# An encoder block with 16384 single-neuron experts: a store moved two loads forward in SyncE's order, and four loads moved from ScalarE's queue to SyncE's

## The chip, the cores and the metric

The kernel runs on one core of a Trainium2 chip. The metric is the device time of one execution in microseconds (us). Each engine of the core works through its own list of instructions in order: TensorE (PE), VectorE (DVE), ScalarE (ACT), GpSimd (POOL) and SyncE (SP). SP computes nothing here; it only waits on semaphores and issues transfers (DMAs), one after the other. A row "SPq" is a transfer's issue on SP, "ACTq" one on ACT's queue.

## What is computed

256 tokens of width 1024 go through one bidirectional encoder block: an input projection, two token mixers (differential attention and neighbourhood attention), gates and an output projection, and then a feed-forward part (PEER) in which every token picks 128 of 16384 experts, each a single neuron. Some seven tenths of the span (793 of 1100 us) go into the feed-forward part, and the change lies there:

```python
def peer_ffn(x, w_query, sub_keys, expert_u, expert_v):
    ...
        q = (xb @ w_query).reshape(TB, PH, 2, PEER_QUERY_DIM // 2)
        s = jnp.einsum('thpd,hpkd->thpk', q, sub_keys).astype(jnp.float32)
        v_half, i_half = lax.top_k(s, K)
        ...
        g = jax.nn.softmax(top_s, axis=-1).astype(xb.dtype)
        u = expert_u[idx]
        a = jax.nn.gelu(jnp.einsum('td,thkd->thk', xb, u), approximate=False)
        return jnp.einsum('thk,thkd->td', g * a, expert_v[idx])
```

The kernel does not gather. It computes gelu(x u) for all 16384 experts, spreads the gates g over a dense matrix G (token by expert, mostly zeros), multiplies the two, and multiplies the product with all of expert_v.

## The kernel before

Weights come in tiles of 128 x 1024 float32 (512 KB), one after the other: 72 tiles of the projections, then 128 tiles of expert_u (here U tiles 0 to 127; in the code t = T_U + i, with T_U = 72), then 128 of expert_v (V tiles). A product of full precision is made of three rounded ones. So each tile passes four stations:

- SP loads it into one of four buffers `raw` (`load`, line 343; it waits until `lo_ready` says that the tile four places earlier has been split, which frees the buffer).
- ACT rounds it into `whis` (`hi`, line 436; a buffer of four, free when PE has finished the tile four places earlier).
- POOL (up to U tile 17) or DVE (from U tile 18: `low_u`, line 883) subtracts to get the remainder `wlos` and raises `lo_ready`.
- PE multiplies: 24 matmuls of 128 x 256 for a U tile, into one of two PSUM banks `pO`.

After a U tile, ACT applies Gelu from `pO` into `ast`, which has two buffers (`gelu`, line 543). SP stores `ast` to the scratch tensor `a_scratch` in HBM (`store`, line 364; it waits for that Gelu by `evac_act`). From the third tile on, `gelu(i)` waits until the store of tile i-2 has landed (`a_stored`), since it writes the same buffer. PE's tile i+2 in turn needs the bank that `gelu(i)` empties.

G is built between the U tiles 39 and 123, in 64 steps on three tiles of every four (`g_step_at`, line 91; `G_LAST` = 123). DVE makes one-hot vectors (`one_hots`, lines 941 and 946), ACT scales a copy of them (`low_hots`, line 561), PE adds two short matmuls after the first half of the tile's chunks and two after the second (`g_tokens`, line 1246), ACT copies the sum from PSUM (line 581) and DVE adds its second half (`add_low`, line 953). On ACT the order within tile i is: `hi(i+3)`, `low_hots`, `gelu(i)`, the copy, `low_hots`. On DVE it is: `one_hots` for the next step, `add_low` of the last step, `low_u(i+2)`, `one_hots`.

SP's order in the U loop is written out: load of tile t, then the store of tile t - `STORE_LAG`, which is 7 (lines 370 to 377). Each waits in turn, so a store cannot go before the load that stands ahead of it.

In the V loop the stored activations come back: `aring`, four buffers, loaded from `a_scratch`. The first four of these loads stand on ACT's queue behind U tile 123 (`first_weights`, line 550), the others on SP's behind each V load (`load_a`). DVE multiplies one with its column of G (`weights`, line 958), ACT rounds the product (`w_hi`, line 597) and DVE takes the remainder (`low`, line 963, `glo_ready`). PE's V tile needs both, and its 12 matmuls of 128 x 512 add into four accumulators. `aring` lies where the buffers of the G steps lay before, so it may only be loaded when these are done.

Of the kernel before, what the change touches and what calls it, by code (L numbers as in the profile page):

```python
# [61 lines left out]
NE_TILES = NK  # L62
# [1 line left out]
T_END = T_V + NE_TILES  # L64
RAW = 4
RING = 4
STORE_LAG = 7
LEAD = 3

UNROLL = 8  # L70
# [6 lines left out]
G_STEPS = T // GTOK  # L77
G_FIRST = 39
G_LAST = G_FIRST + (G_STEPS - 1) // 3 * 4 + (G_STEPS - 1) % 3
# [11 lines left out]
def g_step_at(i):  # L91

    at = i - G_FIRST
    if at < 0 or at % 4 == 3:
        return None
    k = at // 4 * 3 + at % 4
    return k if k < G_STEPS else None
# [40 lines left out]
def act_takings(t):  # L138

    return sum(not evac_engine(x)[0] for x in range(t))  # L140


def build(nc, stream, vrows, const, cols, keys, bias, lamv, gfin, h1_dram, a_dram, out):
    with ExitStack() as top:
# [3 lines left out]
        def sem(name):  # L148
            return top.enter_context(nc.semaphore(name))

        def sbs(stack, name, shape, dt=F32):
            return stack.enter_context(nc.sbuf_tensor(name, shape, dt))
# [71 lines left out]
        with ExitStack() as vphase:  # L224
# [5 lines left out]
            aring = [sbs(vphase, f"aring{s}", [P, T]) for s in range(4)]  # L230
# [79 lines left out]
        g_done = sem("g_done")  # L310
        g_copied = sem("g_copied")
        a_stored = [sem(f"a_stored{s}") for s in range(2)]
        a_landed = [sem(f"a_landed{s}") for s in range(4)]
# [15 lines left out]
        def _(sp):  # L329
# [13 lines left out]
            def load(t, s, row):  # L343

                sp.wait_ge(lo_ready, t - RAW + 1)
                sp.dma_start(raw[s][:], row).then_inc(raw_landed[s], 16)
# [17 lines left out]
            def store(i, s2):  # L364

                sp.wait_ge(evac_act, i + (act_takings(T_U) + 1))
                sp.dma_start(a_dram[i] if isinstance(i, int) else a_dram[bass.ds(i, 1)], ast[s2][:]).then_inc(a_stored[s2], 16)


            for t in range(T_U, T_V):  # L370
                load(t, t % RAW, stream[t])
                if t >= T_U + STORE_LAG:
                    store(t - T_U - STORE_LAG, (t - T_U - STORE_LAG) % 2)
            for s in range(RAW):
                load(T_V + s, s, vrows[s:s + 1])
                i = NE_TILES + s - STORE_LAG
                store(i, i % 2)

            def load_v(i, s):

                row = vrows[i] if isinstance(i, int) else vrows[bass.ds(i, 1)]
                sp.wait_ge(lo_ready, i + (T_V - RAW + 1))
                sp.dma_start(raw[s][:], row).then_inc(raw_landed[s], 16)
# [6 lines left out]
            for s in range(RAW):  # L390
                load_v(RAW + s, s)
                i = NE_TILES + RAW + s - STORE_LAG
                if i < NE_TILES:
# [41 lines left out]
        def _(act):  # L435
# [11 lines left out]
            def hi_at(t):  # L447
                if t < T_END:
                    hi(t, t % RING, landings(t))
# [78 lines left out]
            def take_scores(hp):  # L528

                act.wait_ge(key_scores, hp + 1)  # L530
                act.activation(sc[:, :, hp, :], pS[hp % 2][:, 0:TB * NK].rearrange("p (b k) -> p b k", b=TB), ACT.Copy).then_inc(sbank_taken, 1)
# [11 lines left out]
            def gelu(i):  # L543

                act.wait_ge(tile_done, T_U + i + 1)
                if i >= 2:
                    act.wait_ge(a_stored[i % 2], 16 * (i // 2))
                act.activation(ast[i % 2][:], pO[i % 2][:, 0:T], ACT.Gelu).then_inc(evac_act, 1)  # L548

            def first_weights(s):  # L550

                act.wait_ge(a_stored[s % 2], 16 * (s // 2 + 1))
                act.dma_start(aring[s][:], a_dram[s]).then_inc(a_landed[s], 16)

            def low_hots(u):

                act.wait_ge(hots_ready, u + 1)
                last = None
                for tok in range(GSUB):
                    at = u * GSUB + tok  # L560
                    last = act.activation(ghot[:, u % HOTS, tok, 1, :], ghot[:, u % HOTS, tok, 0, :].bitcast(F32), ACT.Copy,  # L561
                                          scale=routeT[:, 2, at:at + 1])
                last.then_inc(low_hots_ready, 1)

            def u_tile(i):
                hi_at(T_U + i + LEAD)
                ahead = g_step_at(i + 1)
                if ahead is not None:
                    low_hots(2 * ahead)
                if i < 2:  # L570
                    take_scores(HP - 2 + i)
                gelu(i)
                if i == EXP_AT:
                    act.wait_ge(pick_max, 1)
                    act.activation(route[:, :, 2, :, :], route[:, :, 2, :, :], ACT.Exp).then_inc(pick_exp, 1)
                    act.preload_act_table(ACT.Gelu)
                k = g_step_at(i)
                if k is not None:

                    act.wait_ge(g_done, k * 2 + 2)  # L580
                    act.activation(G[:, k * GTOK:(k + 1) * GTOK, :],  # L581
                                   pG[k % 2][:].rearrange("p b (t h i) -> p (b t) h i", t=GSUB, h=2)[:, :, 0], ACT.Copy).then_inc(g_copied, 1)
                if ahead is not None:
                    low_hots(2 * ahead + 1)

            for i in range(G_LAST + 1):
                u_tile(i)

            for s in range(4):
                first_weights(s)  # L590

            def w_hi(i, s):

                act.wait_ge(w_ready, i + 1)
                if not (isinstance(i, int) and i < 2):
                    act.wait_ge(tile_done, i + (T_V - 1))
                act.activation(ghi[s % 2][:], wfull[s % 2][:], ACT.Copy).then_inc(ghi_ready, 1)  # L597

            for i in range(G_LAST + 1, NE_TILES):
                u_tile(i)  # L600
                if i >= NE_TILES - 2:
                    w_hi(i - NE_TILES + 2, i - NE_TILES + 2)
# [784 lines left out]
```

## Time and profile before

| | |
|---|---|
| time, median of 3 runs (lowest to highest) | 1102.28 us (1102.02 to 1104.24) |
| the profiled execution's own time | 1101.85 us |
| its span, first to last instruction | 1100.0 us |
| mean granted TensorE clock | 0.985 |
| busy: PE, PE weight loads, DVE, ACT, POOL | 94%, 86%, 78%, 54%, 20% |
| DMA | 195 GB/s over the span, queue q1 (SP's) 59.6% of 16 engines |
| longest entry of the chain that ended last, beside PE's V loop | DMA a_scratch<-ast, 16% |

The span has four parts: projections, mixers and queries up to 307 us; U tiles without G steps from 307 to 421 us; U tiles with G steps from 421 to 721 us, with the last four U tiles to 734 us; the V loop from 734 us to the end. The matmuls of PE overlap and their ends are modelled, so PE's pace is better read from the distance between the starts of two tiles than from its busy share. A time is read from the profiled execution; what lies around its span is 1.85 us, and its own time is 0.43 us below the median of the runs.

### The profile page before, as it was taken

To read this page: it belongs to the slowest core of one execution; us is meant where nothing else is said; L and a number is where in the kernel's file an instruction comes from. 1 tells how busy PE (TensorE), PEld (TensorE's weight loads), DVE (VectorE), ACT (ScalarE), POOL (GpSimd) and SP (SyncE) were. 2 spreads that over 40 slices of the span, in tenths; PEclk is the share of its full clock that TensorE was granted. 3 is DMA by queue.
4 is the path that set the end of the run, shared out by engine and by line. 5 is a ranking of instruction groups with operands and counts; after the bars stand their busy time and mean duration, and the time that the engine had idled before them with its cause. 6 is when DMAs were issued, how large, how long until landed. Compare 5 with 4: busy or idle time off the path is not lost.

```text
span 1100.0 us, 20666 instructions
## 1 busy us (share of the span) xinstructions
PE 1039.1 (94%) x6950; PEld 943.9 (86%) x6950; DVE 852.8 (78%) x1658; ACT 594.5 (54%) x1089; POOL 218.9 (20%) x94
## 2 busy tenths in 40 slices
PE   5898899889999999999999999999999999999997
PEld 5787899889999999999899899888888888888885
DVE  6988552747999898888788888867777777777776
ACT  5234444254444445777677777755444555444553
POOL 3565556666776000000000000000000000000000
PEclk8899999989999999999999999999999999999999
DMA  8333324444567675665656566688677766776772
GB/s 295 111 135 116 115 97 151 137 174 152 203 195 236 197 244 167 186 190 192 192 183 188 182 195 191 181 256 302 233 239 234 231 231 236 236 236 235 232 230 82
DMA packets 86453, 215.00 MB, mean 195 GB/s; under 512 B 9712, under 2 KB 42864, under 8 KB 85872
## 3 DMA queue, kind: packets, MB, share of 16 engines
q1 hardware_dynamic: 85808, 213.54, 59.6%
q8 instruction: 45, 0.74, 0.3%
q10 hardware_dynamic: 576, 0.52, 0.2%
q14 instruction: 24, 0.20, 0.1%
HBM read 195.15 MB, written 18.87 MB: 195 GB/s over the span
## 4 chain that ended last, share of the span: by engine, by line
PE 51%; DVE 20%; DMA 17%; ACT 8%; issue 3%; SPq 1%; ACTq 0%; DVEq 0%
PE pTT L1297 16%; PE pM L1297 16%; DMA a_scratch<-ast 16%; PE pO L1053 15%; DVE wlos L885 3%; ACT G L581 2%; ACT whis L441 2%; ACT ghot L561 2%; DVE qkT L740 1%; DVE G L953 1%; ACT ast L548 1%; DVE biasm L783 1%; DVE nmx L762 1%; DMA iota<-in_count 1%; DVE mfull L809 1%
## 5 line engine op out<-in xcount | busy, mean ns | idle before, releaser
L441 ACT ACTIVATE whis<-raw 128x1024 fp32r<-128x1024 f32 x328 | 344.6, 1051 | 47.0 <-PE pO L1053 40.6
L422 POOL TENSOR_TENSOR wlos<-raw,whis 128x1024 fp32r<-128x1024 f32 x89 | 218.5, 2461 | 131.7 <-ACT whis L441 131.6
L1053 PE MATMUL pO<-xhi,whis 128*128 128x256 f32 x704 | 200.7, 285 | 3.8 <-ACT ast L548 3.8
L967 DVE TENSOR_TENSOR wlos<-raw,whis 128x1024 fp32r<-128x1024 f32 x125 | 153.2, 1226 | 59.4 <-ACT whis L441 59.4
L1053 PE MATMUL pO<-xhi,wlos 128*128 128x256 f32 x704 | 198.5, 282 | 0.0
L1053 PE MATMUL pO<-xlo,whis 128*128 128x256 f32 x704 | 198.1, 281 | 0.0
L597 ACT ACTIVATE ghi<-wfull 128x256 fp32r<-128x256 f32 x128 | 53.5, 418 | 175.4 <-PE pM L1297 175.4
L885 DVE TENSOR_TENSOR wlos<-raw,whis 128x1024 fp32r<-128x1024 f32 x113 | 137.3, 1218 | 11.1 <-ACT whis L441 11.0
L1272 PE MATMUL pO<-xhi,whis 128*128 128x256 f32 x512 | 143.5, 280 | 1.1 <-ACT ast L548 1.0
L1272 PE MATMUL pO<-xlo,whis 128*128 128x256 f32 x512 | 143.3, 280 | 0.0
L1272 PE MATMUL pO<-xhi,wlos 128*128 128x256 f32 x512 | 143.1, 279 | 0.0
L1053 PEld LDWEIGHTS pO<-xhi,whis 128*128 128x128 f32 x704 | 133.7, 190 | 5.7 <-issue 5.3
L1053 PEld LDWEIGHTS pO<-xlo,whis 128*128 128x128 f32 x704 | 134.0, 190 | 0.0
L1053 PEld LDWEIGHTS pO<-xhi,wlos 128*128 128x128 f32 x704 | 133.7, 190 | 0.0
L548 ACT ACTIVATE ast<-pO 128x256 f32<-128x256 f32 x128 | 48.9, 382 | 139.9 <-DMA a_scratch<-ast 109.5
L1272 PEld LDWEIGHTS pO<-xhi,whis 128*128 128x128 f32 x512 | 96.1, 188 | 1.8 <-issue 1.8
L1272 PEld LDWEIGHTS pO<-xlo,whis 128*128 128x128 f32 x512 | 96.3, 188 | 0.0
L1272 PEld LDWEIGHTS pO<-xhi,wlos 128*128 128x128 f32 x512 | 96.2, 188 | 0.0
L561 ACT ACTIVATE ghot<-ghot,routeT 128x128 fp32r<-128x128 f32 x256 | 88.2, 396 | 8.4 <-DVE ghot L946 8.4
L1053 PE MATMUL pO<-yhi,whis 128*128 128x256 f32 x256 | 78.8, 308 | 11.1 <-DVE ylo L649 8.4
L1297 PE MATMUL pTT<-whis,ghi 128*128 128x512 f32 x256 | 80.7, 395 | 0.0
L1297 PE MATMUL pM<-whis,ghi 128*128 128x512 f32 x256 | 80.6, 394 | 0.0
(187 smaller groups left out, 2055.5 us busy)
## 6 DMA issues: line engine op xcount, KB each, us to landing
raw<-in_stream SPq DMA_DIRECT2D x200, 512.0 KB, 3.7
raw<-in_vrows SPq DMA_DIRECT2D x128, 512.0 KB, 3.5
a_scratch<-ast SPq DMA_DIRECT2D x128, 128.0 KB, 3.8
aring<-a_scratch SPq DMA_DIRECT2D x124, 128.0 KB, 3.3
biasm<-in_bias SPq DMA_DIRECT2D x1, 2048.0 KB, 8.1
xT<-in_xTin SPq DMA_DIRECT2D x2, 512.0 KB, 6.0
keysT<-in_keys SPq DMA_DIRECT2D x1, 1024.0 KB, 5.6
h_scratch<-h1tok SPq DMA_DIRECT2D x1, 1024.0 KB, 6.5
```

The source lines that it names most:

```text
L422: pool.tensor_tensor(wlo[s], raw[s][:], whi[s].bitcast(F32), ALU.subtract).then_inc(lo_ready, 1)
L441: act.activation(whi[s], raw[s][:], ACT.Copy).then_inc(hi_ready, 1)
L548: act.activation(ast[i % 2][:], pO[i % 2][:, 0:T], ACT.Gelu).then_inc(evac_act, 1)
L561: last = act.activation(ghot[:, u % HOTS, tok, 1, :], ghot[:, u % HOTS, tok, 0, :].bitcast(F32), ACT.Copy, scale=routeT[:, 2, at:at + 1])
L581: act.activation(G[:, k * GTOK:(k + 1) * GTOK, :], pG[k % 2][:].rearrange("p b (t h i) -> p (b t) h i", t=GSUB, h=2)[:, :, 0], ACT.Copy).t ...
L597: act.activation(ghi[s % 2][:], wfull[s % 2][:], ACT.Copy).then_inc(ghi_ready, 1)
L740: dve.tensor_tensor(qkT[:, k, :], rtmp[:, 0, :], rtmp[:, 1, :], ALU.add).then_inc(roped, 1)
L885: dve.tensor_tensor(wlo[t % RING], raw[t % RING][:], whi[t % RING].bitcast(F32), ALU.subtract).then_inc(lo_ready, 1)
L967: dve.tensor_tensor(wlo[s], raw[s][:], whi[s].bitcast(F32), ALU.subtract).then_inc(lo_ready, 1)
L1053: last = pe.matmul(dst, st, mv, start=(c == 0 and q == 0), stop=(c == len(terms) - 1 and q == 2))
L1272: last = pe.matmul(pO[i % 2][:, 0:T], st[s][:, c, :], mv[:, c, :], start=c == 0 and q == 0, stop=c == C - 1 and q == 2)
L1297: last = pe.matmul(acc[b][q], st, mv[:, q * 512:(q + 1) * 512], start=first and n == 0, stop=final and n == 2)
```

## The change

`STORE_LAG` becomes 5, so the store of U tile i stands directly behind the load of tile i+5, two loads further forward than before. The four first loads of `aring` leave ACT's queue and stand on SP's, behind the store of U tile 123, with a wait for all G steps (`g_done`) ahead of them. The buffers, the sizes and the number of transfers stay.

```diff
-STORE_LAG = 7
+STORE_LAG = 5
...
                 i = NE_TILES + s - STORE_LAG
                 store(i, i % 2)
+                if i == G_LAST:
+
+                    sp.wait_ge(g_done, 2 * G_STEPS)
+                    for q in range(4):
+                        sp.wait_ge(a_stored[q % 2], 16 * (q // 2 + 1))
+                        sp.dma_start(aring[q][:], a_dram[q]).then_inc(a_landed[q], 16)
...
-            def first_weights(s):
-
-                act.wait_ge(a_stored[s % 2], 16 * (s // 2 + 1))
-                act.dma_start(aring[s][:], a_dram[s]).then_inc(a_landed[s], 16)
-
...
-            for i in range(G_LAST + 1):
-                u_tile(i)
-
-            for s in range(4):
-                first_weights(s)
-
...
-            for i in range(G_LAST + 1, NE_TILES):
+            for i in range(NE_TILES):
                 u_tile(i)
```

SP, at the start of the U loop, before (the rows are the loads of U tiles 4 to 7, the store of tile 0, the load of tile 8 and the store of tile 1; the number behind a name is the buffer):

```order
L346 DMA raw0<-in_stream 128x1024 [waits lo_ready]
L346 DMA raw1<-in_stream 128x1024 [waits lo_ready]
L346 DMA raw2<-in_stream 128x1024 [waits lo_ready]
L346 DMA raw3<-in_stream 128x1024 [waits lo_ready]
L367 DMA a_scratch<-ast0 128x256 [waits evac_act]
L346 DMA raw0<-in_stream 128x1024 [waits lo_ready]
L367 DMA a_scratch<-ast1 128x256 [waits evac_act]
```

SP at the same place, after:

```order
L346 DMA raw0<-in_stream 128x1024 [waits lo_ready]
L346 DMA raw1<-in_stream 128x1024 [waits lo_ready]
L367 DMA a_scratch<-ast0 128x256 [waits evac_act]
L346 DMA raw2<-in_stream 128x1024 [waits lo_ready]
L367 DMA a_scratch<-ast1 128x256 [waits evac_act]
L346 DMA raw3<-in_stream 128x1024 [waits lo_ready]
L367 DMA a_scratch<-ast0 128x256 [waits evac_act]
```

The store of tile 0 now follows the load of tile 5 instead of 7, and from there on load and store alternate with this smaller distance through all 128 tiles; the load of tile i+6 now stands behind the store of tile i.

SP, at the end of the U loop, before (from the load of V tile 0; the stores are those of U tiles 121 to 125, the row of L388 is the load of activation 4):

```order
L346 DMA raw0<-in_vrows 128x1024 [waits lo_ready]
L367 DMA a_scratch<-ast1 128x256 [waits evac_act]
L346 DMA raw1<-in_vrows 128x1024 [waits lo_ready]
L367 DMA a_scratch<-ast0 128x256 [waits evac_act]
L346 DMA raw2<-in_vrows 128x1024 [waits lo_ready]
L367 DMA a_scratch<-ast1 128x256 [waits evac_act]
L346 DMA raw3<-in_vrows 128x1024 [waits lo_ready]
L367 DMA a_scratch<-ast0 128x256 [waits evac_act]
L383 DMA raw0<-in_vrows 128x1024 [waits lo_ready]
L367 DMA a_scratch<-ast1 128x256 [waits evac_act]
L388 DMA aring0<-a_scratch 128x256 [waits w_ready,a_stored0]
```

SP at the same place, after (the stores are those of U tiles 123 to 126):

```order
L346 DMA raw0<-in_vrows 128x1024 [waits lo_ready]
L367 DMA a_scratch<-ast1 128x256 [waits evac_act]
L383 DMA aring0<-a_scratch 128x256 [waits a_stored0,g_done]
L383 DMA aring1<-a_scratch 128x256 [waits a_stored1]
L383 DMA aring2<-a_scratch 128x256 [waits a_stored0]
L383 DMA aring3<-a_scratch 128x256 [waits a_stored1]
L346 DMA raw1<-in_vrows 128x1024 [waits lo_ready]
L367 DMA a_scratch<-ast0 128x256 [waits evac_act]
L346 DMA raw2<-in_vrows 128x1024 [waits lo_ready]
L367 DMA a_scratch<-ast1 128x256 [waits evac_act]
L346 DMA raw3<-in_vrows 128x1024 [waits lo_ready]
L367 DMA a_scratch<-ast0 128x256 [waits evac_act]
```

The four loads of `aring` now stand between the store of U tile 123 and the load of V tile 1.

ACT around the end of U tile 123, before:

```order
L548 ACTIVATE ast1<-pO1 128x256 [waits a_stored1,tile_done]
L581 ACTIVATE G<-pTT 128x512 [waits g_done]
L553 DMA aring0<-a_scratch 128x256 [waits a_stored0]
L553 DMA aring1<-a_scratch 128x256 [waits a_stored1]
L553 DMA aring2<-a_scratch 128x256 [waits a_stored0]
L553 DMA aring3<-a_scratch 128x256 [waits a_stored1]
L441 ACTIVATE whis<-raw3 128x1024 [waits tile_done,raw_landed3]
L548 ACTIVATE ast0<-pO0 128x256 [waits a_stored0,tile_done]
```

ACT at the same place, after:

```order
L554 ACTIVATE ast1<-pO1 128x256 [waits a_stored1,tile_done]
L582 ACTIVATE G<-pTT 128x512 [waits g_done]
L447 ACTIVATE whis<-raw3 128x1024 [waits tile_done,raw_landed3]
L554 ACTIVATE ast0<-pO0 128x256 [waits a_stored0,tile_done]
L447 ACTIVATE whis<-raw0 128x1024 [waits tile_done,raw_landed0]
```

The four issues are gone from ACT, and nothing else there has moved (the line numbers shift by the length of the new code).

## Rows read from the trace of the kernel before

**Rows 1.** Busy time by stretch: length, then us (and count) by engine, clock, DMA, GB/s.

```profile
307.00:421.29 114.29, 112.16 (x949) 111.47 (x948) 105.49 (x302) 55.26 (x83) 37.04 (x16) 1.00 0.70 218
421.29:721.04 299.75, 284.39 (x2298) 274.27 (x2297) 248.74 (x530) 217.61 (x489) 0.00 (x0) 1.00 0.60 185
721.04:734.46 13.42, 11.72 (x99) 11.43 (x97) 6.91 (x8) 6.41 (x11) 0.00 (x0) 1.00 0.88 284
740.00:1080.00 340.00, 340.00 (x1459) 272.76 (x1458) 266.18 (x366) 169.46 (x244) 0.00 (x0) 1.00 0.71 238
```

**Rows 2.** Timeline of PE: starts of U tiles 58 to 62.

```profile
489.34 0.28 PE L1053 MATMUL pO<-xhi,whis 128*128 128x256 f32 x1
...
492.17 0.28 PE L1272 MATMUL pO<-xhi,whis 128*128 128x256 f32 x1
...
495.85 0.28 PE L1272 MATMUL pO<-xhi,whis 128*128 128x256 f32 x1
...
499.83 0.28 PE L1272 MATMUL pO<-xhi,whis 128*128 128x256 f32 x1
...
503.12 0.28 PE L1053 MATMUL pO<-xhi,whis 128*128 128x256 f32 x1
```

**Rows 3.** Waits of the engines, whole span: us in total, times, longest.

```profile
ACT ast L548 <- DMA a_scratch<-ast: 109.5, 79, 3.4
...
DVE G L953 <- ACT G L581: 53.9, 63, 3.1
```

**Rows 4.** Waits of SP's queue, whole span: us in total, times, longest.

```profile
SPq L346 <- DVE wlos L885: 277.5, 110, 6.9
...
SPq L367 <- ACT ast L548: 12.3, 33, 1.4
```

**Rows 5.** Chain that ended last, one turn: start, us, what.

```profile
449.31 0.60 ACT G L581
...
449.94 0.69 DVE G L953
450.63 1.14 DVE wlos L885
...
451.79 0.33 SPq L346
...
452.17 3.72 DMA a_scratch<-ast
```

**Rows 6.** Timeline of ACT and of SP: Gelu of tile 59, its store.

```profile
497.93 0.38 ACT L548 ACTIVATE ast<-pO 128x256 f32<-128x256 f32 x1 [1.00 <-DMA a_scratch<-ast]
498.21 0.59 ACT L581 ACTIVATE G<-pTT 128x512 f32<-128x512 f32 x1
498.69 0.69 ACT L561 ACTIVATE ghot<-ghot,routeT 128x128 fp32r<-128x128 f32 x2
...
501.06 0.43 SPq L367 DMA_DIRECT2D a_scratch<-ast  x1
```

**Rows 7.** Timeline of PE: start of U tile 23.

```profile
374.46 0.35 PE L1053 MATMUL pO<-xhi,whis 128*128 128x256 f32 x1 [1.29 <-ACT ast L548]
```

**Rows 8.** Timelines, end of the U loop: Gelu 125, U tile 127, glo, V tile 0.

```profile
730.86 0.38 ACT L548 ACTIVATE ast<-pO 128x256 f32<-128x256 f32 x1 [3.43 <-DMA a_scratch<-ast]
...
731.39 0.36 PE L1053 MATMUL pO<-xhi,whis 128*128 128x256 f32 x1 [1.70 <-ACT ast L548]
...
733.82 0.42 DVE L963 TENSOR_TENSOR glo<-wfull,ghi 128x256 fp32r<-128x256 f32 x1 [0.37 <-ACT ghi L597]
...
734.39 0.47 PE L1297 MATMUL pTT<-whis,ghi 128*128 128x512 f32 x1
```

**Rows 9.** Issue to landing, 421 to 721 us: tile raw, then tile a_scratch.

```profile
DMA to landing us min/median/max: 3.6/3.7/4.9
...
DMA to landing us min/median/max: 3.5/3.7/5.3
```

**Rows 10.** Issues by line: the first loads of aring, KB each, us to landing.

```profile
aring<-a_scratch ACTq DMA_DIRECT2D x4, 128.0 KB, 3.1
```

## The prediction, made blind

> **What bounds the kernel now.** I read the busy times by stretch first [rows 1]. In the V loop PE is busy 340.00 of 340 us: nothing but PE counts there, and time won earlier is kept. In the stretch with G steps (421 to 721 us) matmuls are busy 284 of 300 us, which looks like a full engine. The tile starts say otherwise [rows 2]. Tile 58, without a G step, takes 492.17 - 489.34 = 2.83 us, and tile 61, with one, 503.12 - 499.83 = 3.29 us; tiles 59 and 60, of the same work as 61, take 3.68 and 3.98. Tile 58's 2.83 is 24 matmuls one every 0.118 us without a gap, and 61's four short matmuls add the rest; so 2.83 and 3.29 are PE's floor. The four tiles 58 to 61 take 503.12 - 489.34 = 13.78 us, their floor is 3 x 3.29 + 2.83 = 12.70.
>
> What PE waits for is found with the waits [rows 3]: the longest one of the stretch is ACT's, 109.5 us in 79 Gelus that waited for the store of the same `ast` buffer. PE hardly waits for Gelu itself; it waits for what ACT does behind it (the copy of G, the scaled one-hots), which starts late with it. Why the store is late stands in SP's own waits [rows 4]: the load ahead of it waited 277.5 us for DVE's split, the store 12.3 us for its Gelu. The chain shows the loop that this closes [rows 5]: copy of G 0.60, `add_low` 0.69, split of tile i+3 1.14, issue of load i+7 0.33, store i 3.72 until it has landed, and only then Gelu i+2. With the Gelu (0.38) and the gaps between them one turn takes 6.9 to 7.0 us for two tiles: that is the present pace, 13.8 to 14 us for four. Tile 59 in full [rows 6]: its Gelu ends at 498.31, its store goes at 501.06, 2.75 us later.
>
> **The store two loads earlier, with G steps.** Store i now stands behind load i+5, which waits for the split of tile i+1. DVE makes that two tiles before the split of i+3, so it is done before Gelu i. The store then goes as soon as the Gelu ends, and the 2.75 us are gone. What is left of the loop: Gelu 0.38, issue, landing 3.72, next Gelu; some 4.3 us for two tiles, against PE's floor of 2.83 + 3.29 = 6.12 or more. Even the longest landing, 5.3 us [rows 9], fits. The other loop (copy, `add_low`, split i+1, load i+5, store i, Gelu i+2) keeps its 7 us but now spans four tiles, of 12.70 us.
>
> So I ask what is late next. ACT: from the start of a Gelu to the start of the `ghot` pair is 498.69 - 497.93 = 0.76 us, the pair ends some 0.7 later [rows 6], so 1.5 to 1.7 us after a tile's end the one-hots for the next tile's second half are there; PE wants them after that tile's 24 matmuls, 3.05 us. DVE: 248.74 us of work for 85 tiles is 2.93 us per tile, ACT 217.61/85 = 2.56 [rows 1], against a mean floor of 3.18. DVE would be 92% busy. In order on DVE, three G tiles in a row cost a little more than PE's floor and the fourth gives it back; its split of tile i+2 stays over 3 us ahead of PE. So PE is the bound and the stretch comes to its floor: 64 x 3.29 + 21 x 2.83 = 270.0 us instead of 299.75 [rows 1]. **Gain 29.8 us.** A lower end comes from PE's weight loads, idle 299.75 - 274.27 = 25.5 us.
>
> The Trainium skill ("Perfetto Trace Analysis", section Identifying the Most-Contended Engine) says the same of the measures: weight-load busy time shows TensorE's headroom and matmul busy time does not. By it the sum would have 25.5 us here, by matmul busy time 15.4; the tile starts of this trace say 29.8, and I go by them.
>
> **The store two loads earlier, before the G steps.** From 307 to 350 us nothing waits for stores for long. From 353 us on DVE's routing work delays splits, stores go late, Gelus with them, and PE waits for the bank, as tile 23 does, 1.29 us [rows 7]. With the store behind its Gelu this goes; ACT's two table loads near tile 20 are then the one thing there that comes close to PE. Weight loads are idle 114.29 - 111.47 = 2.8 us in this stretch [rows 1]. **Gain 2.8 us**, bounds 0 and 2.8.
>
> **What the moved store puts behind itself.** Load i+6 waited for a split alone; it now stands behind store i, hence behind Gelu i. Before 350 us this makes it nearly a tile (2.83 us) later. It is issued about 1 us after the end of tile i (Gelu 0.38, store issue 0.43, gaps), lands 3.7 us later, at most 4.9 [rows 9], and ACT rounds it after tile i+2, 5.7 us after tile i. With the longest landing the rounding is some tenths late, and PE wants the tile three tiles after that. With G steps the split and the Gelu come at about the same time, so the load hardly moves. **Cost 0.** SP issues 0.33 + 0.43 us per tile, far below 3.18.
>
> **The four loads on SP.** ACT loses four issues, which are not on PE's path: 0. On SP they wait for `g_done`, which tile 123 raises before its own Gelu is over, so this wait is met when the store of tile 123 goes. Behind them in SP's order stand the load of V tile 1 and the stores from 124 on: later by four issues, about 1.7 us at the store's 0.43. The first product of DVE needs `aring` 0: issue some 0.9 us after tile 123's end, landing after 3.1 us on ACT's queue [rows 10], longer behind a load, so by 4 to 5.5 us; ACT rounds that product after tile 126, about 9 us. PE's V tile 0 needs `glo` 0: Gelu 126, the rounding and DVE's 0.42 end about 1.4 us after tile 126, and tile 127 takes 2.83. Before, `glo` 0 started at 733.82 for a V tile 0 at 734.39 [rows 8]: the margin is small today since the Gelus are late, and grows. **Cost 0**, at most the 1.7 us.
>
> **The last four U tiles.** Gelu 125 waited for the store of 123 (it started at 730.86), and PE's tile 127 for that, 1.70 us [rows 8]. Four tiles should take 11.3; they took 734.39 - 721.04 = 13.35. **Gain 2.0 us.**
>
> **Sum.** 29.8 + 2.8 + 2.0 = 34.6 us, from the profiled execution's 1101.85: 1067.25; the median of the runs is 0.43 above it: 1067.7. That is the floor, and no row prices the small misses (a slow landing, an engine a tenth late). I add 1.3 us for them: **1069.0 us**.
>
> **Rivals.**
> - *DVE becomes the bound.* It is at 92% in the new pace, and today `add_low` waits 53.9 us for the copy, 0.86 per step [rows 3]. If half of that stays, DVE needs 248.7 + 27 us and with its other hand-offs some 280 for the stretch: 10 us less gain, **1078 us** (1073 to 1084). For it: three G tiles in a row are above PE's floor on DVE. Against it: the copy will follow PE's tile, not a store.
> - *Slower: loads starve behind the store.* If raw loads land late because SP waits for the Gelu first, a loop of six tiles closes: Gelu, store issue, load issue, landing, rounding, split, tile; some 6.9 us and the landing. It passes PE's floor (19.1 us for six) from a landing of 12.2 us, and today's pace (21.2) from 14.3; at 16 us the 85 tiles take 3.82 each and the kernel **1127 us**. Against it: the longest landing is 4.9 [rows 9]. The Trainium skill ("Perfetto Trace Analysis", section DMA Optimizations) speaks for it: it advises one engine for inputs and another for outputs, and this change ties them closer on one. No row here shows a harm from that.
> - *The handover gives back.* If `aring` or V tile 1 comes late, PE waits at 734 us for up to the four issues and a landing's spread: **1071 us**.
> - *It doesn't do what it says.* If the store still waits for the load ahead of it, as in today's rows, nothing changes: **1102 us**. The split of i+1 would have to be as late as that of i+3; the order on DVE excludes it.
>
> **Chances.** The floor with small misses (1067 to 1073) 0.66, DVE bound 0.22, handover 0.05, no change 0.03, loads starve 0.04. The range 1066.5 to 1079 holds the first, the third and over half of the second. About 0.2% (2.2 us) is what a measurement of this kernel can tell from no change: faster 0.93, same 0.03, slower 0.04.
>
> **What would show it.** In the profile after: a Gelu's wait for stores near nothing; the store's issue within 0.2 us of its Gelu; SP's stores, not its loads, waiting; tile starts 3.29 and 2.83 apart from 421 us on; V tile 0 at about 700 us; the V loop unchanged. It is wrong if four tiles still take over 13.2 us, and then the wait that PE's `g_tokens` or DVE's `add_low` shows names the cause; or if ACT's rounding waits for `raw`.

## The result and the profile after

| | before | after |
|---|---|---|
| time, median (lowest to highest), 4 runs each on one chip | 1103.12 us (1102.02 to 1104.24) | 1057.64 us (1055.03 to 1057.67) |
| ratio, 95% interval | | 0.9582 (0.9563 to 0.9601) |
| the profiled execution's own time | 1101.85 us | 1057.65 us |
| its span | 1100.0 us | 1055.8 us |
| mean granted TensorE clock | 0.985 | 0.989 |

The kernel became faster, as forecast, but by 44.2 us between the two profiled executions where the forecast's sum had 34.6 and the forecast itself 33. The time lies 9 us below the range.

Busy time by stretch of the kernel after (columns as in [rows 1]), cut at the starts of U tiles 0, 39 and 124 and of V tile 0:

```profile
306.44:417.66 111.22, 111.22 (x949) 111.22 (x948) 105.36 (x302) 55.35 (x83) 37.06 (x16) 1.00 0.68 222
417.66:679.58 261.92, 261.92 (x2298) 261.92 (x2297) 246.48 (x530) 220.68 (x490) 0.00 (x0) 1.00 0.65 215
679.58:690.47 10.89, 10.89 (x99) 10.89 (x98) 7.07 (x9) 6.16 (x10) 0.00 (x0) 1.00 0.81 272
697.00:1037.00 340.00, 340.00 (x1459) 273.95 (x1458) 265.15 (x365) 169.72 (x243) 0.00 (x0) 1.00 0.71 239
```

PE and its weight loads now fill each stretch of the U loop from end to end. Against [rows 1] and the tile starts of before, the stretch before the G steps went from 114.29 to 111.22 us (3.1 gained), that with them from 299.75 to 261.92 (37.8), the last four tiles from 13.35 to 10.89 (2.5). The V loop is as it was. The remaining 0.8 us lie ahead of tile 0 and in the tail.

Starts of U tiles 58 to 62 on PE after, for [rows 2]:

```profile
476.54 0.28 PE L1048 MATMUL pO<-xhi,whis 128*128 128x256 f32 x1
...
479.26 0.28 PE L1267 MATMUL pO<-xhi,whis 128*128 128x256 f32 x1
...
482.46 0.28 PE L1267 MATMUL pO<-xhi,whis 128*128 128x256 f32 x1
...
485.66 0.28 PE L1267 MATMUL pO<-xhi,whis 128*128 128x256 f32 x1
...
488.86 0.28 PE L1048 MATMUL pO<-xhi,whis 128*128 128x256 f32 x1
```

The tile without a G step takes 2.72 us and every one with a G step 3.20. Four tiles take 12.32 us, where they took 13.78, and where the forecast put PE's floor at 12.70. PE went below what the forecast called its floor. That is the surprise of this case.

The waits of the engines after (whole span; us in total, times, longest), for [rows 3]:

```profile
ACT ast L554 <- PE pO L1048: 69.5, 60, 2.0
...
ACT ast L554 <- PE pO L1267: 20.9, 41, 0.8
DVE G L948 <- ACT G L582: 16.2, 40, 2.1
...
ACT whis L447 <- DMA raw<-in_stream: 4.1, 4, 2.3
```

The Gelu's 109.5 us of waits for the store are gone: Gelu now waits for PE, as it should. `add_low` waits 16.2 us for the copy of G instead of 53.9. SP's queue (whole span), for [rows 4]:

```profile
SPq L367 <- ACT ast L554: 265.6, 128, 6.4
...
SPq L346 <- DVE wlos L880: 1.3, 4, 0.6
```

The waits have changed places. The store now waits for its Gelu (265.6 us, harmless), the load behind it for almost nothing: 1.3 us for DVE's split and, in the U loop, 2.8 us for POOL's. Tile 59 on ACT and SP, for [rows 6]:

```profile
482.42 0.38 ACT L554 ACTIVATE ast<-pO 128x256 f32<-128x256 f32 x1
482.70 0.60 ACT L582 ACTIVATE G<-pTT 128x512 f32<-128x512 f32 x1
...
482.83 0.34 SPq L367 DMA_DIRECT2D a_scratch<-ast  x1
483.22 0.43 SPq L346 DMA_DIRECT2D raw<-in_stream  x1
```

Its Gelu ends at 482.80 and the store goes at 482.83, 0.03 us later; it was 2.75. From issue to landing in the stretch with G steps, first the stores, then the raw loads, for [rows 9]:

```profile
DMA to landing us min/median/max: 1.7/2.2/3.3
...
DMA to landing us min/median/max: 3.4/3.9/5.5
```

The store lands in 2.2 us, where it took 3.7. The load behind it takes 0.2 us more. The handover, for [rows 8], on SP, DVE and PE:

```profile
679.95 0.34 SPq L367 DMA_DIRECT2D a_scratch<-ast  x1
680.41 1.81 SPq L383 DMA_DIRECT2D aring<-a_scratch  x4
...
689.66 0.42 DVE L958 TENSOR_TENSOR glo<-wfull,ghi 128x256 fp32r<-128x256 f32 x1
...
690.46 0.39 PE L1292 MATMUL pTT<-whis,ghi 128*128 128x512 f32 x1
```

The four loads of `aring` go right behind the store of tile 123 and take SP 1.81 us; `glo` 0 ends 0.38 us ahead of V tile 0, and PE has no gap there.

### The profile page after: what moved, and what is told of

Same layout as the page of the kernel before. It is cut to its first block, busy times and chain, and to the rows that moved or that the text cites. A ratio compares the mean times of both kernels' runs of the same rounds, so it can differ in the third digit from the quotient of the medians.

```text
span 1055.8 us, 20667 instructions
## 1 busy us (share of the span) xinstructions
PE 1010.9 (96%) x6950; PEld 928.6 (88%) x6950; DVE 848.7 (80%) x1658; ACT 597.7 (57%) x1089; POOL 218.9 (21%) x94
## 4 chain that ended last, share of the span: by engine, by line
PE 86%; DVE 10%; issue 1%; ACT 1%; DMA 1%; SPq 0%; DVEq 0%; ACTq 0%
PE pO L1048 30%; PE pTT L1292 17%; PE pM L1292 17%; PE pO L1267 17%; PE pTT L1241 1%; PE pSS L1241 1%; DVE qkT L735 1%; DVE nmx L757 1%; DVE biasm L778 1%; DMA iota<-in_count 1%; DVE mfull L804 1%; PE pM L1137 1%; DVE gates L655 1%; ACT prob L512 1%; PE pSS L1213 1%
## 5 line engine op out<-in xcount | busy, mean ns | idle before, releaser
L1048 PE MATMUL pO<-xhi,whis 128*128 128x256 f32 x704 | 198.8, 282 | 0.0
L1048 PE MATMUL pO<-xlo,whis 128*128 128x256 f32 x704 | 196.7, 279 | 0.0
L1267 PE MATMUL pO<-xhi,whis 128*128 128x256 f32 x512 | 141.3, 276 | 0.0
L1267 PE MATMUL pO<-xlo,whis 128*128 128x256 f32 x512 | 141.3, 276 | 0.0
L1292 PE MATMUL pTT<-whis,glo 128*128 128x512 f32 x256 | 80.7, 395 | 0.0
L1292 PE MATMUL pM<-whis,glo 128*128 128x512 f32 x256 | 80.7, 395 | 0.0
```

What stands on the lines that cost most here:

```text
L1048: last = pe.matmul(dst, st, mv, start=(c == 0 and q == 0), stop=(c == len(terms) - 1 and q == 2))
L1267: last = pe.matmul(pO[i % 2][:, 0:T], st[s][:, c, :], mv[:, c, :], start=c == 0 and q == 0, stop=c == C - 1 and q == 2)
L1292: last = pe.matmul(acc[b][q], st, mv[:, q * 512:(q + 1) * 512], start=first and n == 0, stop=final and n == 2)
```

## Experiments

Three questions: which half of the change brings the gain, by which loop of waits, and why PE went below the forecast's floor. All ratios are to the kernel before, run on the same chip beside each kernel. Where a stretch is named, its time is that of the profiled execution. Each edit is against the kernel after, unless it is said otherwise. In the 14 profiles tile 0 starts anywhere from 302.84 to 308.99 us, so single times of kernels with the same U loop can lie 6 us apart by what stands ahead of it.

### The loads of aring on SP alone

```diff
-STORE_LAG = 5
+STORE_LAG = 7
```

> The other half of the change alone: STORE_LAG 7, the four first aring loads on SP behind the store of tile 123. Theory: the G stretch is as in the kernel before; the aring loads now wait for a late store of tile 123, so DVE's first products come about 3 us later and V tile 0 starts 0 to 4 us later: 1102 to 1107 us. Rival (the move of the loads frees ACT and carries part of the gain beyond the forecast): 1090 to 1098 us.

Measured: 1104.97 us, ratio 1.0015 (0.9991 to 1.0039). Its waits (whole span; us in total, times, longest) are much like those of the kernel before:

```profile
ACT ast L554 <- DMA a_scratch<-ast: 124.8, 91, 3.3
DVE G L948 <- ACT G L582: 58.2, 64, 3.2
```

The second half of the change alone does nothing that can be measured.

### The store two loads forward alone

The first loads of `aring` stay on ScalarE's queue. Against the kernel before it is one number:

```diff
-STORE_LAG = 7
+STORE_LAG = 5
```

> The first half of the change alone: STORE_LAG 5, the four first aring loads on ACT's queue as before. Theory: all of the gain, within 1.5 us of the changed kernel (1056 to 1059). Rival (the move of the loads carries the 10 us beyond the forecast): 1066 to 1069 us.

Measured: 1056.85 us, ratio 0.9572 (0.9539 to 0.9606). Its waits of SP's queue (whole span) are those of the kernel after, and no Gelu waits for a store:

```profile
SPq L367 <- ACT ast L548: 274.7, 128, 6.4
...
SPq L346 <- DVE wlos L885: 1.1, 3, 0.6
```

The whole gain is the store's place. That the loads cost nothing on SP, as forecast, follows from this run and the one above.

### How far forward: six, four and three loads

Each is one number (with the few lines at the end of the U loop that keep the order whole):

```diff
-STORE_LAG = 5
+STORE_LAG = 6
```

> STORE_LAG 6 in the changed kernel, nothing else. Theory (loop): what counts is over how many tiles the 7 us loop copy of G, add_low, split, load, store, Gelu is spread; with 6 it is three tiles (9.1 us or more at PE's pace), so it does not bind, tiles with a G step start 3.2 us apart, and the time is within 2 us of the changed kernel (1057 to 1060). Rival (each place forward is worth its share): half of the gain, about 1080 us.

> STORE_LAG 4 in the changed kernel (the four aring loads again behind the store of tile 123), nothing else. Theory (loop): store i now holds back load i+5, whose rounding stands on ACT ahead of Gelu i+2. A loop closes over two tiles: Gelu 0.38, store issue 0.34, load issue 0.43, landing 3.9, rounding 1.05, some 6.2 us. Two tiles with G steps take 5.9 to 6.4 at PE's pace, two without 5.7: the tiles before 415 us become 3.1 us each, the others stay near 3.2 to 3.4; 1065 to 1085 us. Rival (earlier stores never hurt): 1057 us.

> The store of tile i stands three loads behind its own load instead of five, so SyncE issues it ahead of the load of tile i+4. Theory (the forecast's rival of a load that starves behind a store decides where a loop closes: store of i, load of i+4, halves of i+4, Gelu of i+4): over four raw buffers the load can't start before the store of tile i has been issued, which waits for Gelu i, so the halves of tile i+4 come at least landing 3.4 + rounding and difference about 2.3 us behind Gelu i, in which TensorE has only the tiles up to i+3 to do: it takes about one tile (Gelu i to halves i+4 to matmuls i+4 within four tiles, 4 x 2.72 = 10.9 us) and still closes, 1056 to 1075 us with TensorE waiting now and then. Rival (the order of the loads themselves is what limits): with the next load late by one more tile the U loop runs at 3.5 us or more a tile, 1140 us and above.

Measured: six, 1057.29 us, ratio 0.9585 (0.955 to 0.9621), the same as five. Four, 1074.16 us, ratio 0.9737 (0.9703 to 0.977). Three, 1425.82 us, one run. Three is a plain miss for what I wrote: the theory's 1056 to 1075 us is far off, and the rival's open "1140 us and above" holds the time only by the letter, since it was priced from 3.5 us a tile. Its waits (whole span), and one turn at three loads on SP and ACT:

```profile
ACT whis L447 <- DMA raw<-in_stream: 458.8, 127, 5.8
```

```profile
601.27 0.34 SPq L367 DMA_DIRECT2D a_scratch<-ast  x1
601.66 0.43 SPq L346 DMA_DIRECT2D raw<-in_stream  x1
...
605.37 1.06 ACT L447 ACTIVATE whis<-raw 128x1024 fp32r<-128x1024 f32 x1 [3.05 <-DMA raw<-in_stream]
...
606.91 0.36 ACT L554 ACTIVATE ast<-pO 128x256 f32<-128x256 f32 x1
...
607.30 0.34 SPq L367 DMA_DIRECT2D a_scratch<-ast  x1
```

The loop is one tile long, not four. Store i goes, then the load of tile i+4; it lands 3.71 us later; ACT rounds it, and the next Gelu stands behind that rounding in ACT's order; then the next store. One turn takes 607.30 - 601.27 = 6.03 us, and a tile with it: ACT's own order closes the loop long before PE does. (From 420 to 900 us of this run PE is busy 331 of 480 us and its granted clock averages 0.84. The turn shown has no wait for PE, so the clock does not set it.) This is the loop by which the change could have gone wrong. At three loads it spans one tile, at four two, at five three. Two tiles are 5.7 to 6.6 us at the paces of [rows 2], just at the 6.03 us; three are 8.2 us or more, so five loads leave over 2 us of room, and a sixth brings nothing more. (The room at five is worked out from this turn; no run made a landing longer.) At four the room is gone, as the waits of the stretch with G steps show (421.69 to 692.99 us):

```profile
ACT whis L446 <- DMA raw<-in_stream: 26.9, 47, 1.8
```

and the stretches of it:

```profile
306.12:421.69 115.57, 112.82 (x949) 111.90 (x948) 105.22 (x298) 55.75 (x82) 36.74 (x16) 1.00 0.70 213
421.69:692.99 271.30, 270.64 (x2298) 270.29 (x2297) 249.14 (x534) 223.20 (x490) 0.00 (x0) 1.00 0.67 208
```

The second row holds more than late loads. PE stands still only 0.66 us there by its busy time, and yet the stretch takes 9.4 us more than at five loads: its tiles take 2.83 and 3.29 us again where nothing is waited for. PE is busy; it is slower. A kernel further below, without a stop, takes 270.14 us for the same tiles at that pace, so some 8 of the 9.4 us are the pace and about 1 the late loads. (Of the other 7 us, 4.3 are in the stretch ahead and the rest behind it, where V tile 0 waits 1.34 and 0.70 us for `glo`.)

### Stores on ScalarE's queue

The Trainium skill, in the section that the forecast cites ("Perfetto Trace Analysis", section DMA Optimizations), says that it may make sense to give inputs one engine and outputs another. This kernel does so.

```diff
-                if t >= T_U + STORE_LAG:
-                    store(t - T_U - STORE_LAG, (t - T_U - STORE_LAG) % 2)
...
+                act.wait_ge(evac_act, i + (act_takings(T_U) + 1))
+                act.dma_start(a_dram[i], ast[i % 2][:]).then_inc(a_stored[i % 2], 16)
```

> The changed kernel, but every store of an activation tile is issued from ScalarE's queue, behind the Gelu that makes the tile; SyncE's queue then holds loads alone. Theory (what the change is worth is that the store goes at the Gelu's end and no longer behind a load's wait; which queue it has is not the point): the store goes as early, loads go earlier, but ScalarE gets an issue of 0.3 to 0.4 us a tile on top of 135.1 us of work per 52 tiles (2.60 us a tile); 2.9 to 3.0 against TensorE's mean 3.08 us leaves next to nothing, so some hand-offs come late: 1058 to 1080 us. [...]

Measured: 1057.60 us, ratio 0.9579 (0.9553 to 0.9604), the same as the kernel after, and just under the 1058 where my range began. Its DMA issues (KB each, median us to landing):

```profile
raw<-in_stream SPq DMA_DIRECT2D x200, 512.0 KB, 3.8
...
a_scratch<-ast ACTq DMA_DIRECT2D x128, 128.0 KB, 3.6
```

The loads no longer wait for a Gelu, the loop of the last section doesn't exist, and the time is the same: what limited the kernel before was the store that stood behind a load's wait. The three places tried that free it without closing a shorter loop (five loads, six loads, ACT's queue) are equally good, on one queue or on two. Neither harm nor gain of sharing a queue shows here.

### One stop of TensorE

In the stretch with G steps the trace of before has a stop of PE in nearly every round of four tiles, that of after none in the whole U loop. In the trace of before, a tile without a G step takes 2.83 us (24 matmuls at 118 ns) between those stops; in the trace of after 2.72 (113 ns). Both traces have 118 ns from tile 0 to tile 36 and 113 ns right behind the six transposes ahead of tile 37. Before goes back to 118 ns at its first stop behind them, at 428.8 us, and of the 128 groups of matmuls that can be read from there to 721 us one is at 113 ns. After stays at 113 ns to the end of the U loop. The granted clock is 1.00 in both. PE before, at the six transposes, the starts of tiles 38 and 39 (2.72 us apart) and that stop:

```profile
415.19 0.82 PE L1253 MATMUL pM<-cst,route 128*128 128x128 f32 x6
...
418.57 0.28 PE L1053 MATMUL pO<-xhi,whis 128*128 128x256 f32 x1
...
421.29 0.28 PE L1272 MATMUL pO<-xhi,whis 128*128 128x256 f32 x1
...
428.82 0.48 PE L1246 MATMUL pTT<-ghot,hot 128*128 128x256 f32 x2 [1.21 <-ACT ghot L561]
```

So the next edits stop PE in the kernel after, or put short matmuls ahead of a tile.

```diff
+            STOPS = (42,)
             for i in range(NE_TILES):
+                if i in STOPS:
+                    pe.wait_ge(evac_act, act_takings(T_U) + i)
```

> The changed kernel with one wait more: before U tile 42 TensorE waits until the Gelu of tile 41 has ended, so it stops once, early in the stretch with the G tiles. Theory (the pace of 113 ns from one matmul of 256 columns to the next, which the changed kernel has from tile 37 to the end of the U loop, is a state that lasts only while TensorE doesn't stop; after a stop it is drawn anew, and it came out at 118 ns after nearly all the stops of the kernel before): the stop itself costs 0.5 to 1 us, and if 118 ns is drawn the 82 tiles behind it cost 24 x 4.4 ns = 0.106 us each more, 8.7 us: 1066 to 1068 us, U tile starts 2.83 us apart. Rival (the pace belongs to the stretch, to what the other engines do there, and not to TensorE's own stops): 113 ns comes back at once, 1058 to 1059 us.

Measured: 1062.36 us median of 4 runs from 1059.89 to 1065.75, ratio 0.9621 (0.9589 to 0.9653). The profiled execution, at 1060.72, stopped once and kept 113 ns; of the 3.1 us that it lies above the kernel after, 2.6 stand ahead of tile 0 and 0.5 in the stretch with the stop. No forecast of mine covers the whole of it: the stop didn't bring back 118 ns in the run that I can see, and the two runs of 1064.00 and 1065.75 may have gone otherwise, which no trace shows. It doesn't tell the theories apart.

### Twelve stops, twice

```diff
+            STOPS = (6, 12, 18, 24, 30, 50, 60, 70, 80, 90, 100, 110)
```

> The changed kernel with twelve such waits, before U tiles 6, 12, 18, 24, 30 and 50, 60 up to 110: each stops TensorE until the Gelu of the tile ahead has ended. It samples the pace after a stop. Theory (drawn anew at a stop): the pace changes only at these places and at the six transposes ahead of tile 37, and both paces, 113 and 118 ns, are seen; twelve stops at 0.5 to 1 us are 6 to 12 us, and up to 60 slow tiles in place of fast ones 6 us, less what fast stretches ahead of tile 37 give back (up to 3 us): 1062 to 1076 us. Rival (the pace belongs to the stretch): 118 ns ahead of tile 37 and 113 ns behind it whatever the stops, 1064 to 1070 us.

> The kernel with twelve stops of TensorE once more, unchanged. Theory (the pace after a stop is drawn by chance in each execution): another pattern of 113 and 118 ns than the first profile had, where it was 118 behind tiles 6, 12, 24, 60, 80, 100 and the six transposes, and 113 behind 18, 30, 50, 70, 90, 110; time 1062 to 1076 us. Rival (the program determines the pace: the same instructions give the same pattern): the same pattern, 1065 to 1069 us.

Measured: 1067.08 us, ratio 0.9656 (0.9624 to 0.9688), and the same kernel again 1066.71, ratio 0.9665 (0.9624 to 0.9706). Both times lie in the ranges of theory and rival alike; only the profiles decide. PE in the first of the two profiles, at the stop ahead of tile 50 and the starts of tiles 54 and 55, then at the stop ahead of tile 60 and the starts of tiles 62 and 63:

```profile
456.74 0.38 PE L1048 MATMUL pO<-xhi,whis 128*128 128x256 f32 x1 [0.24 <-ACT ast L554]
...
469.17 0.28 PE L1048 MATMUL pO<-xhi,whis 128*128 128x256 f32 x1
...
471.89 0.28 PE L1270 MATMUL pO<-xhi,whis 128*128 128x256 f32 x1
...
487.81 0.38 PE L1270 MATMUL pO<-xhi,whis 128*128 128x256 f32 x1 [0.24 <-ACT ast L554]
...
494.51 0.28 PE L1048 MATMUL pO<-xhi,whis 128*128 128x256 f32 x1
...
497.34 0.28 PE L1270 MATMUL pO<-xhi,whis 128*128 128x256 f32 x1
```

The same tile, of the same stretch, takes 2.72 us behind one stop and 2.83 behind the next. Both paces exist on either side of tile 37. So the pace doesn't belong to the stretch: that rival falls. In both profiles it changed only at a stop or at the six transposes. The values behind tiles 6, 12, 18, 24, 30 were 118, 118, 113, 118, 113 in the first profile and 113, 118, 113, 118, 113 in the second; behind 50 to 110 they alternated from 113 in both. The same program gave two patterns ahead of tile 37 and one behind it: neither plain chance nor the program alone.

### Short matmuls without a stop

```diff
...
+            TURNS = {4: 1, 8: 2, 12: 3, 16: 4, 20: 5, 24: 6, 28: 1, 32: 2}
             for i in range(NE_TILES):
+                if i in TURNS:
+                    probe_turns(TURNS[i])
```

`probe_turns(n)` issues n idle transposes of 128 columns. In the second kernel it is three idle matmuls of 128 columns each, at the 16 tiles 4, 8 up to 32 and 50, 60 up to 120.

> The changed kernel with idle 128-column transposes put between U tiles, of which nothing comes: 1 ahead of tile 4, 2 ahead of 8, 3 ahead of 12, 4 ahead of 16, 5 ahead of 20, 6 ahead of 24, 1 ahead of 28, 2 ahead of 32. TensorE does not stop for them. Theory (a matmul group of another width shifts how weight load and matmul interleave, and so can change the pace without a stop, as the six transposes ahead of tile 37 changed it from 118 to 113 ns in the changed kernel and from 113 to 118 ns in the kernel whose first loads alone were moved): the pace changes at some of the eight places. 24 transposes at about 0.1 us are 2.4 us; with half of tiles 4 to 36 at 113 ns, 1.8 us come back; if the last draw, at tile 37, is 118 ns, the 91 tiles behind it cost 9.6 us: 1058 to 1070 us. Rival (the pace belongs to the stretch): 118 ns up to tile 37 and 113 ns behind it, 1060 us.

> The changed kernel with three idle matmuls of 128 columns ahead of each of the U tiles 4, 8 up to 32 and 50, 60 up to 120, 48 in all, of which nothing comes; TensorE does not stop for them. Three such were what changed the pace at tile 12 in the kernel with idle transposes. Theory (a group of another width draws the pace anew): it changes at some of the 16 places and at tile 37, with no fixed pattern; 48 x 0.11 = 5.3 us more work, and half of the 128 tiles at 118 ns: 1061 to 1069 us. Rival (three always switch the pace to the other value): it alternates from place to place, with the six at tile 37 as two or no switches, 1061 to 1066 us. Second rival (once TensorE runs at 113 ns without a stop, only a stop ends that): 113 ns from some early place to the end, 1056 to 1060 us.

Measured: the first 1068.82 us, ratio 0.9667 (0.9643 to 0.9691), the second 1070.58, ratio 0.9705 (0.9677 to 0.9733). The second lies above all three of its forecasts, none of which had 118 ns for nearly the whole loop. In the first the three at tile 12 brought 113 ns, the four at 16 brought 118 back, and neither the others nor the six of the program ahead of tile 37 changed anything, so that the rest of the U loop ran at 118. In the second the six ahead of tile 37 brought 113 and the three at tile 50 brought 118 for good. Three don't switch it each time, and 113 ns, once there, doesn't last by itself: both rivals fall. The stretches of the first kernel, cut at tiles 0, 39 and 124:

```profile
307.11:420.77 113.66, 113.66 (x974) 113.66 (x973) 106.13 (x303) 55.70 (x84) 37.03 (x16) 1.00 0.70 217
420.77:690.91 270.14, 270.14 (x2299) 270.14 (x2297) 247.20 (x529) 220.70 (x490) 0.00 (x0) 1.00 0.67 208
```

The second row settles the size of the miss. With the store in its new place, no stop of PE and 118 ns, tiles 39 to 123 take 270.14 us. The forecast had 270.0. At 113 ns they take 261.92.

### Two stops, to gain by it

If an interruption mostly switches the pace, two well-placed stops should give 113 ns from tile 4 on.

> The changed kernel with two stops of TensorE, before U tiles 4 and 39, each until the Gelu of the tile ahead has ended. In the two profiles with twelve stops the pace changed to its other value at 21 of 24 stops (not at tiles 6 and 12 of the first, nor at 50 of neither: there it changed), and the six transposes ahead of tile 37 changed it too. Theory (such an interruption mostly switches the pace): 118 ns, from tile 4 on 113, from tile 37 on 118, from tile 39 on 113 again; the 33 tiles from 4 to 36 give back 33 x 0.106 = 3.5 us, the two stops cost 0.75 each, the result 2.0 us under the changed kernel: 1054 to 1057 us. Rival (what comes after an interruption isn't to be foreseen): one of the stretches comes out at 118 ns; if it is the long one, from tile 39, 9 us are lost: 1060 to 1068 us.

(The count in that text is wrong; the pace changed at 22 of the 24 stops, not at tiles 6 and 12 of the first profile.) Measured: 1067.26 us, five runs from 1066.99 to 1067.46, ratio 0.9677 (0.9653 to 0.9702), in the rival's range. Nothing switched: 118 ns behind tile 4, behind the six transposes and behind tile 39, to the end. The second stop in its profile:

```profile
418.47 0.39 PE L1270 MATMUL pO<-xhi,whis 128*128 128x256 f32 x1 [0.47 <-ACT ast L554]
```

and PE's rows of the stretch from 480 to 640 us, first of this kernel, then of the kernel after:

```profile
480.00:640.00 160.00, 160.00 (x1362) 160.00 (x1361) 147.16 (x317) 131.04 (x291) 0.00 (x0) 1.00 0.66 207
```

```profile
480.00:640.00 160.00, 160.00 (x1405) 160.00 (x1405) 150.72 (x326) 135.12 (x299) 0.00 (x0) 1.00 0.65 214
```

PE is busy all of the time in both, at a granted clock of 1.00, and does 1362 matmuls in one and 1405 in the other. The theory of a switch falls. No version came out that beats the kernel after by more than the runs' spread.

## Why the prediction was right and wrong

**The bound and the loop: right.** The store behind a load that waits for DVE, Gelu behind the store, PE behind what ACT does after Gelu: with the store's place alone changed, each of these waits went [rows 3, 4, 6] as forecast, store 0.03 us behind its Gelu, SP's loads without a wait, and the gain with them. The first part of the change is all of it (0.9572 alone), the second nothing (1.0015). One reading was loose: the rows of waits are of the whole span, and the prediction took them for the stretch with G steps, where the Gelus waited 74.5 us for stores and SP's loads 229.0 us for DVE. No term of the sum rests on them.

**The step that failed: PE's floor.** "2.83 and 3.29 are PE's floor" was read from two tiles of before [rows 2], both at 118 ns from matmul to matmul. That is a pace that PE had there, and not its fastest: the trace of before itself shows 113 ns, for some hundred matmuls behind the six transposes ahead of tile 37 (tile 38 takes 2.72 us there), which I had not read. The term for the stretch with G steps, 29.8 us, is what one gets at 118 ns (299.75 - 270.14 = 29.6 in the kernel with idle transposes); the kernel after ran at 113 and got 37.8. The 8.1 us between are 64 x 0.09 + 21 x 0.11 = 8.07. The same holds for the last four tiles: 2.0 forecast, 2.5 measured, 4 x 0.11 of it from the pace. The forecast's 1067.25 before its reserve is about the time of this change without the faster pace: the kernel with two stops, at 118 ns throughout, takes 1067.26. That the two agree to a hundredth is luck, since the two stops of 0.47 us are in it.

**The reserve of 1.3 us: wrong in sign.** I added it for small misses, and there were none: PE has no gap from tile 0 to V tile 0.

**Before the G steps: right.** 2.8 us forecast, 3.1 measured, a little over the upper bound of 2.8. Tiles 37 and 38 are at 113 ns in both traces, so the pace changes nothing there.

**Landings.** The sum kept 3.7 us for the store; in its new place it took 2.2. This changed nothing, since the loop had room.

**Handover: right.** No wait of PE; 0.38 us between `glo` 0 and V tile 0.

**The rivals.** DVE is 246.48 / 261.92 = 94% busy and doesn't bound; its wait for the copy fell to 16.2 us. Loads that starve behind the store is a real mechanism, but I had given it the wrong loop: six tiles through PE, deciding at a landing of 12 us. The loop that closes first goes through ACT's order and spans three tiles. Its turn was 6.03 us with a landing of 3.71, so 2.3 us beside the landing; three tiles at 8.2 us would be passed from a landing of some 5.9. The longest was 5.5. The forecast's "some tenths late" at the longest landing was nearer than its rival's price; with one load less of distance the kernel lost 16.5 us, some 8 of them by the pace, with two 368.

**The measure of room.** The Trainium skill ("Perfetto Trace Analysis", section Identifying the Most-Contended Engine) names the weight loads' busy share as one of two measures of TensorE. By it 25.5 us were to be had in the stretch [rows 1]; tile starts said 29.8, and at the pace of that trace 29.6 was right. The gain of 37.8 was visible in neither, and the measure does not show the pace: weight loads are busy all of the stretch in the kernel after, at 113 ns, and in the kernel with idle transposes, at 118.

**The range** ended 0.75 us under the forecast's sum, because I took a floor for certain. No term of it allowed for PE being faster than it was.

## What to carry to other kernels

In a queue that waits in order, look for the instruction that is ready and stands behind one that isn't; then bound how far forward it may go by the shortest loop that its new place closes, through every engine's own order and not only through the busiest engine. Before you call the distance of two tile starts the engine's floor, look through the whole trace for the shortest such distance of the same work: an engine that is 100% busy can still have two paces. Here the kernel without stops gained 8 to 9 us of its 44 beyond what the stops had cost, and small edits elsewhere in PE's stream lost that again.

## What the runs showed of TensorE that I had not expected

The same 256-column matmuls, each behind its weight load, start every 113 ns or every 118 ns (24 of them 2.72 or 2.83 us), at a granted clock of 1.00 in both cases. In all kernels profiled here, but for the one with three loads (its granted clock in the U loop was below 1.00), the pace changed only where PE stopped or a group of matmuls of another width went by, and held for hundreds of matmuls otherwise. The four matmuls of a G step, called short ahead, are no such group: they have 256 columns too and take 0.48 us, 3.20 less 2.72. After the six transposes ahead of tile 37 it went from 118 to 113 ns in before, in after and in the kernels with six loads, the store alone, the store on ScalarE's queue, one stop and idle matmuls; from 113 to 118 with the loads alone and in both profiles with twelve stops; it stayed at 118 with idle transposes, with two stops and, behind a stop of PE of 1.50 us, with four loads. The short stops of the kernel before left it at 118 in 127 of 128 groups that could be read. What in an interruption decides stays open: not the stretch (both paces in either), not the number of short matmuls (six did all three things), not the program alone (two patterns from one program). That the second part of the gain, the 8.1 us, is a lasting property of this order of instructions is therefore not shown; it was there in the profile of the kernel after and in those of its three nearest relatives (six loads, the store alone, the store on ScalarE's queue), each with 261.92 us for the tiles 39 to 123. By their times the executions without a profile went the same way: all 16 of the four kernels lie between 1054.05 and 1059.51 us, the five of the kernel with two stops, at 118 ns, between 1066.99 and 1067.46.
